# Spreading 128 expert dot products over two searches and a table, with gather buffers that hold no early chunks

## The reference, cut to what matters

```python
q = (xc @ w_query).reshape(C, PEER_HEADS, 2, PEER_HALF)
sc = jnp.einsum('thpd,hpnd->thpn', q, sub_keys)
top_s, top_i = lax.top_k(sc, PEER_TOPK)
cand_s = (top_s[:, :, 0, :, None] + top_s[:, :, 1, None, :]).reshape(C, PEER_HEADS, PEER_TOPK * PEER_TOPK)
cand_i = (top_i[:, :, 0, :, None] * PEER_NKEYS + top_i[:, :, 1, None, :]).reshape(...)
best_s, best_pos = lax.top_k(cand_s, PEER_TOPK)
experts = jnp.take_along_axis(cand_i, best_pos, axis=-1)
gates = jax.nn.softmax(best_s, axis=-1)
u, vv = expert_down[experts], expert_up[experts]
act = jax.nn.gelu(jnp.einsum('cd,chkd->chk', xc, u), approximate=False)
return jnp.einsum('chk,chkd->cd', gates * act, vv)
```

## Time and profile before

| | us |
|---|---|
| median of 3 runs | 1519.17 |
| lowest and highest | 1518.54, 1522.5 |
| profiled execution, its own time | 1524.2 |
| its span | 1522.4 |

### The profile page before, as it was taken

The page is one execution under the profiler, slowest core; times in us unless marked ns, Lnnn a source line. Parts: engine busy times, 40 slices in busy tenths (PEclk is TensorE's granted clock), DMA queues, the critical chain, the costliest instruction groups (busy, mean ns, idle before and its releaser), DMA issues. The chain is left out here.

```text
span 1522.4 us, 24797 instructions
## 1 busy us (share of the span) xinstructions
PE 1409.8 (93%) x8327; PEld 1212.7 (80%) x8327; DVE 993.1 (65%) x2325; ACT 636.8 (42%) x1256; POOL 205.5 (13%) x170
## 2 busy tenths in 40 slices
PE   7998989997896758999999999999999999989998
PEld 4665689997796658777777777789999999659994
DVE  4666569977996567566666666665555555256761
ACT  2433242017750005433333333356665665326651
POOL 0000164325876420000000000000000000000000
PEclk9999999999997988999999999999999999999999
DMA  8330187898999992365656556485554443236630
GB/s 299 133 137 1 46 333 263 314 386 307 404 409 409 409 403 85 99 191 181 191 188 185 192 182 191 138 249 176 178 153 153 152 152 111 91 89 193 183 90 28
DMA packets 145527, 307.17 MB, mean 202 GB/s; under 512 B 39968, under 2 KB 89632, under 8 KB 143904
## 3 DMA queue, kind: packets, MB, share of 16 engines
q1 hardware_dynamic: 127008, 238.93, 46.9%
q0 software_dynamic: 18432, 67.12, 11.5%
HBM read 304.73 MB, written 1.29 MB: 201 GB/s over the span
## 5 line engine op out<-in xcount | busy, mean ns | idle before, releaser
L1331 PE MATMUL plain_u<-whole,ring 128*128 128x128 f32 x1760 | 218.3, 285 | 34.6 <-DMA ring<-in_downT 34.6
L1331 PEld LDWEIGHTS plain_u<-whole,ring 128*128 128x128 f32 x1760 | 210.8, 200 | 40.2 <-DMA ring<-in_downT 40.0
L1882 ACT ACTIVATE hT_high<-ring 128x1024 fp32r<-128x1024 f32 x128 | 135.8, 1061 | 224.8 <-PE experts_acc L247 223.7
L245 PE MATMUL experts_acc<-hT_high,experts_wh 128*128 128x512 f32 x512 | 204.5, 399 | 1.5 <-DVE hT_low L1898 1.5
L246 PE MATMUL experts_acc<-hT_low,experts_wh 128*128 128x512 f32 x512 | 203.2, 397 | 0.0
L247 PE MATMUL experts_acc<-hT_high,experts_wl 128*128 128x512 f32 x512 | 203.2, 397 | 0.0
L1682 DVE CUSTOM_DVE_ANT_0 table<-table,h_row 128x1024 f32<-128x1024 f32 x128 | 152.3, 1223 | 45.1 <-DMA table<-in_down_rows,select_expert 41.6
L1459 POOL DMA_INDIRECT table<-in_down_rows,select_expert x128 | 161.6, 1262 | 145.1 <-DVE select_u L1682 101.4
L1898 DVE TENSOR_TENSOR hT_low<-ring,hT_high 128x1024 fp32r<-128x1024 f32 x128 | 156.9, 1226 | 27.4 <-ACT hT_high L1882 27.4
L245 PE MATMUL mix_a_pj<-mix_a_wh,hT_high 128*128 128x384 f32 x368 | 129.1, 351 | 0.0
L245 PEld LDWEIGHTS experts_acc<-hT_high,experts_wh 128*128 128x128 f32 x512 | 96.6, 189 | 35.2 <-issue 7.5
(11 more groups left out here) (393 smaller groups left out, 2601.9 us busy)
## 6 DMA issues: line engine op xcount, KB each, us to landing
ring<-in_up SPq DMA_DIRECT2D x128, 512.0 KB, 3.5
ring<-in_downT SPq DMA_DIRECT2D x110, 512.0 KB
mix_raw<-in_wa SPq DMA_DIRECT2D x46, 768.0 KB, 6.2
block_w_raw<-in_w SPq DMA_DIRECT2D x16, 768.0 KB, 6.2
mix_raw<-in_wb SPq DMA_DIRECT2D x16, 768.0 KB, 6.7
ring<-in_route SPq DMA_DIRECT2D x16, 576.0 KB, 5.2
table<-in_downT SPq DMA_DIRECT2D x18, 512.0 KB, 6.0
wo<-in_wo SPq DMA_DIRECT2D x4, 1024.0 KB, 7.9
```

What stands on the lines that cost most here:

```text
L245: pe.matmul(out, lhs[0], rhs[0], start=start, stop=False, skip_group_check=True)
L1331: mm = pe.matmul(self.u[g % 2][:, i * P:(i + 1) * P], rows[:, k, :], self.h[:, k, P:SEQ], start=k == 0, stop=k == KD - 1, skip_group_check ...
L1882: act.activation(uh[b % 2], raw_u[b], ACT.Copy).then_inc(u_high, 1)
```

## The change

It has four parts.

1. `FREE` = 12: none of the 12 gather buffers holds an early chunk. `EARLY` becomes 6 (was 18), the POOL waits for chunks in the first 12 gathers are gone, and SP issues none of the chunks ahead of the weights (`first` is 0 instead of 6), then one behind each of the first six weights. Chunks 6 and 7 go into the two free ring buffers behind the last weight.
2. `AHEAD` = 60 (was 56) chunks before the slot transposes, so 20 instead of 24 beside the first table.
3. The dot products are placed anew: the two choices come as before; 6 dot products stand in the first search itself, 29 in the second, 3 after the gates (38 in all up to the transposes, where there were 16), then 1 and 2 in turn in the 17 rounds of the table (25, where there were 51), and 65 in the last ten rounds (where there were 61). All use the same code; `dots` now takes a count.
4. `begun` follows (63), and with it the pacing of SP.

```diff
-EARLY = GATHERS + 6
+FREE = 12
+EARLY = GATHERS - FREE + 6
-AHEAD = 56
+AHEAD = 60
-DOTS_FIRST, DOTS_HALVES, DOTS_INDEX, DOTS_TURN, DOTS_GROUP = 4, 1, 3, 2, 3
+DOTS_FIRST, DOTS_LISTS, DOTS_PAIRS, DOTS_INDEX, DOTS_TURN = 2, 2, 3, 5, 3
+DOTS_SEARCH = 3 * DOTS_FIRST + 2 * DOTS_PAIRS + 4 * DOTS_LISTS + 3 * DOTS_INDEX + DOTS_TURN
...
-    begun = DOTS_FIRST + 4 * DOTS_HALVES + 2 * DOTS_INDEX + DOTS_TURN + DOTS_GROUP * (GROUPS + 1)
+    begun = DOTS_SEARCH + sum(1 + g % 2 for g in range(GROUPS + 1))
...
-            first = EARLY - (HP - NW)
+            first = max(0, EARLY - (HP - NW))
...
-                chunks.load(sp, first + hp - NW)
+                if first + hp - NW < EARLY:
+                    chunks.load(sp, first + hp - NW)
...
-                if s < GATHERS:
-                    pool.wait_ge(chunks.projected, EARLY_ROWS + s + 1)
-                else:
+                if FREE <= s < GATHERS:
+                    pool.wait_ge(chunks.projected, EARLY_ROWS + s - FREE + 1)
+                elif s >= GATHERS:
...
-            for n in range(2):
-                for h in range(4 * n, 4 * n + 4):
-                    halves(0, h)
-                    if n == 0:
-                        halves(1, h)
-                pairs(0, n)
-                indices(0, n)
-                choose(n)
-            at = DOTS_FIRST
-            dots(0, at)
-            for n in range(2):
-                for h in range(4 * n, 4 * n + 4):
-                    if n == 1:
-                        halves(1, h)
-                        dots(at, at + DOTS_HALVES)
-                        at += DOTS_HALVES
-                pairs(1, n)
-                indices(1, n)
-                dots(at, at + DOTS_INDEX)
-                at += DOTS_INDEX
+            for h in range(4):
+                halves(0, h)
+                halves(1, h)
+            pairs(0, 0)
+            indices(0, 0)
+            choose(0)
+            at = 0
+            for h in range(4, HEADS_P):
+                halves(0, h)
+                if h > 4:
+                    at = dots(at, DOTS_FIRST)
+            pairs(0, 1)
+            indices(0, 1)
+            choose(1)
+            at = dots(at, DOTS_INDEX)
+            pairs(1, 0)
+            at = dots(at, DOTS_PAIRS)
+            indices(1, 0)
+            at = dots(at, DOTS_INDEX)
+            for h in range(4, HEADS_P):
+                halves(1, h)
+                at = dots(at, DOTS_LISTS)
+            pairs(1, 1)
+            at = dots(at, DOTS_PAIRS)
+            indices(1, 1)
+            at = dots(at, DOTS_INDEX)
...
-                dots(at, at + DOTS_GROUP)
-                at += DOTS_GROUP
+                at = dots(at, 1 + g % 2)
...
-            left = SLOTS - at
+            left = SLOTS - begun
...
-                         for b in range((GATHERS, EARLY - GATHERS)[t])] for t in range(NT)]
+                         for b in (range(FREE, GATHERS), range(EARLY - GATHERS + FREE))[t]] for t in range(NT)]
```

More of the change, by code:

```diff
@@ L1675, in choose, with dots @@
                 dve.tensor_copy(expert[:, at], number[:, at]).then_inc(chosen, 1)
-            def dots(lo, hi):
-                for s in range(lo, hi):
+            def dots(lo, n):
+                for s in range(lo, lo + n):
                     b = s % GATHERS
@@ L1682, in dots @@
                     dve.tensor_tensor_reduce(gathered[b], gathered[b], h_row[:], 1.0, 0.0, ALU.mult, ALU.add, u[:, s:s + 1]).then_inc(dotted, 1)
+                return lo + n
             def digit(t, n, part):
@@ L1771, in _ @@
             last.then_inc(cols_ready, 1)
-            dots(at, at + DOTS_TURN)
-            at += DOTS_TURN
+            at = dots(at, DOTS_TURN)
             dve.wait_ge(cols_turned, 2)
@@ L1790, in _ @@
                 join(g, late_gelu[g - first])
-            left = SLOTS - at
+            left = SLOTS - begun
             for n, g in enumerate(range(middle, last)):
-                dots(at + left * n // (last - middle), at + left * (n + 1) // (last - middle))
+                at = dots(at, left * (n + 1) // (last - middle) - left * n // (last - middle))
                 join(g, late_gelu[(g - first) % WAITING])
```

## The result

The changed kernel takes 1535.86 us (median of 4 runs, 1532.82 to 1539.37); the kernel before, run beside it, takes 1520.15 (4 runs). The ratio is 1.0099, 95% interval 1.0077 to 1.0121: it is slower by 15 us, and outside the range (1509 to 1529). The profiled execution took 1532.82 us with a span of 1531.0. Its end lies only 8.6 us behind the one of before, while the last gather lies 13.9 us behind; the medians differ by 15.7, so the last gather is the better marker, and the profiled execution of before took some 5 us more than the changed one behind it.

What follows compares the result with a forecast made beforehand. Bound by empty DMA time before the last gather: 19.6 + 3 + 14 + 6.5 + 1 = 44.1 us against 44.8, so that gather lands 0.9 us earlier and the median is 1518.3 us, no change; range 1509 to 1529.

Steps and rivals of the forecast that it cites:

- What bounds the kernel: Up to the last gather: empty DMA time decides, 44.8 us before the change, with 342.5 us of transfers in both kernels.
- The queries: Queries and first search: they end 10 us earlier, first gather at 237.5, but 19.6 us of DMA empty instead of 13.7.
- I count 3 us empty ... From 248 us on both queues have work: After the first gather: 3 us of DMA empty (bounds 1.5 and 5), then gathers and chunks both queue from 248 us.
- TensorE ... reaches 60 at about 370: Before the slot transposes: TensorE finishes 60 chunks at 369.5 us against 347.4, so the first table starts 22 us later.
- The search's end: VectorE's search with 35 dot products takes 107 us, ending near 343, and near 352 with the gates and 3 more dots.
- The first table: The 15 table groups take 61 us, 63 up to the joins instead of 83.8; joins start at 445.3.
- The rival with 4.7 us a group: First table shrinks too little: 70.5 us instead of 61, kernel at 1527.8; chance 0.30, including 0.02 for the low clock.
- 14 us are empty: Beside the first table: 57.6 us of transfers wanted in 71.7 us, so 14 us of DMA time empty.
- 6.5 at the joins: At the joins, with buffers full and chunk 88 waiting for 69 dots: 6.5 us of DMA empty (bounds 0 and 9).
- The account of gains and losses: Up to the last gather: 44.1 us empty against 44.8, so it lands at 570.4 instead of 571.3, 0.9 us earlier.
- The later start eats the whole gain of the shorter table: First table: starts 22 us later, is 20.8 us shorter, so the joins start at 445.3 against 444.1.
- The rule of the low clock: TensorE waiting for DMA before its matmuls runs at the low clock, reaching its 60th chunk some 40 us later; chance 0.02.

Runs made afterwards that it cites:

- x_pace: The changed kernel, but each of the first 12 gathers (gather s) waits until chunk s has been multiplied: ratio 1.0066 to the kernel before.
- x_mid_four: The kernel before with 4 of 12 gather buffers free of early chunks and 26 (not 16) dot products before the slot transposes: ratio 0.9899.
- x_free: The kernel before with only the 12 gather buffers freed of early chunks; old dot products and 56 chunks: ratio 1.0014.
- x_four: The kernel before with 4 gather buffers freed of early chunks and nothing else: ratio 0.9968.
- x_burst: The kernel before, but the first twelve gathers all wait until 14 chunks are multiplied and then go back to back: ratio 1.0074.
- x_dots: The kernel before with only the new places of the dot products (38 before the slot transposes): ratio 1.0008.
- the pair: The changed kernel with 56 instead of 60 chunks before the slot transposes: ratio 1.0060; with the first 12 gathers also paced by chunks, 1.0043.

## Why the prediction was wrong, point by point

- **What bounds the kernel** was right: the empty DMA time before the last gather accounts for when that gather comes, within 1.7 us in 16 of 17 kernels. My count of it for the changed kernel was wrong: 44.1 us up to the last gather, where it is some 58 (56.1 to 550 us and 2.2 behind).
- **The queries** (19.6 us empty to 237, and the 3 that follow) were right: 21.8 to 240. The 19.6 is a slip, 34 from 53 leaves 19; two more, without effect, are the 373.6 (240 + 133.3 is 373.3) and the 5.4 us a group, where the rows have 5.2. The weights' wait went, and the first gather came within 1.3 us.
- **"I count 3 us empty ... From 248 us on both queues have work"** failed. 240 to 290 us holds 8.2 more empty us. From 244 to 264 us gathers alone pass: SyncE issues no chunk between 235.4 and 264.65 us, though by TensorE's rows chunk 6, whose buffer it waits for, is through at about 249.4 (in x_pace at 248.6, and there SyncE issues at 248.74). 3 of the 8.2 are the crawl: x_pace has 5.0. With 240 to 355 us filled I had 90 transfers; x_pace moved 23.65 + 21.15 MB, 85.4 transfers, the changed kernel 83.
- **"TensorE ... reaches 60 at about 370", of which I took 369.5, is the step that failed: 380.74.** Of the 11.2 us, 3.6 are the crawl (377.14 in x_pace). For the rest compare x_pace at 355 us: I had 8.5 chunks to go at 1.79 us each, that is, with the gather buffers already full. Ten were to go, and the buffers weren't full: six came at 2.50 us (354.89 to 369.90) and only the last four at 1.81. The 1.5 chunks make 2.7 us and the slower six 4.3; with 0.7 by which I rounded down, 11.3. My own count had 50 gathers moved by 355 us; 45 had been (23.65 MB).
- **The search's end** was late too (348.6 at L1762 instead of near 343), harmless, since VectorE then waited 19.70 us.
- **The first table** was right: 61.6 us from first to last eviction (61), so 4.11 us apart, joins 2.35 us later. The rival with 4.7 us a group, to which I gave the slower side, did not happen; the kernel is slower by another way.
- **"14 us are empty" in the table, and 6.5 at the joins**, together with 1 of small losses 21.5, were 28.5 between 372 us and the last gather. The split was off in both places. From 372 to the first join at 457.6 us 25.4 us are empty: 1.6 up to the transposes, 8.9 up to the first eviction and 15.0 beside the table. Behind it there are 3 instead of 7.5. The 11.4 us too many in the table's stretch match the 11.2 by which it starts late: the gather buffers were full before the transposes (the last gather ahead of them is issued at 363.21, and from 373.5 chunks come at full speed), and in the 24 us until a dot product frees one, only the few chunks that TensorE takes can be moved.
- **The account of gains and losses.** "The later start eats the whole gain of the shorter table" took the 22 us as exact; at 33 the balance is gone. The last gather landed 14.7 us later than my 570.4; the joins account for 12.3 of it (457.6 instead of 445.3). As a ledger: 21.8 + 8.2 + 25.4 + 3 = 58.4 empty, against my 44.1.
- **The rule of the low clock**, to which I gave 0.02, did not apply: 290 to 350 us, where TensorE waits half a microsecond for nearly each chunk, shows a granted clock of 1.00. The section that the prediction names in the Trainium skill (TensorE: Matmul & The Clock Gate, "Loop structure matters more than you think") shows a long wait ahead of every matmul going with the low clock, and the prediction left the "long" out; these waits are short.

The general fault: I treated three parts as adding up in one ledger and weighed none of them alone. Once all buffers are full, every transfer that the parts have brought ahead of the table is missing beside it, and each puts off the table's start, while its own demand (20 chunks and 25 gathers, 57.6 us of transfers) can't fill the 85.6 us from 372 up to the joins.

## What to carry to other kernels

Where transfers bound a stretch, count its empty microseconds by window and spread demand so that no window runs dry; what fills a hole early is missing from a later window once all buffers are full. When a queue runs ahead, ask at what rate the other side is served *until* the buffers are full, not after. Of a resource that can be freed in steps, try the small step: 4 buffers of 12 gave more than 12. And weigh the parts of a change alone and in pairs before trusting their sum.

## What the runs showed of the hardware that was not expected

Several engines can stand still for "issue" behind a run of gathers, with their data there. In the changed kernel, from 244 to 264 us, gathers alone are moved, and a single instruction packet passes; in x_pace three pass beside them (queues, packets, MB, share of the engines' time; the changed kernel, then x_pace):

```profile
q0 software_dynamic: 1983, 7.23, 98.1%
q14 instruction: 1, 0.01, 0.1%
```

```profile
q0 software_dynamic: 1299, 4.74, 65.0%
q1 hardware_dynamic: 659, 2.43, 31.7%
q8 instruction: 1, 0.02, 0.3%
q14 instruction: 2, 0.02, 0.2%
```

x_mid_four, without a crawl, has the gathers at 92.3% in the same 20 us, and three instruction packets:

```profile
q0 software_dynamic: 1812, 6.62, 92.3%
q8 instruction: 2, 0.03, 0.6%
q14 instruction: 1, 0.01, 0.1%
```

So it is not the presence of gathers but, it seems, their backlog: GpSimd issues one per 1.24 us at best (1.35 on average for the 18 up to 261.67 us), and at 363 GB/s (245 to 264 us) one takes 1.44 us, just the time from one burst of matmuls to the next. How long it lasts goes with how many gathers are issued in one run. With 12 unpaced and 38 dots, which free buffers for 6 gathers more, it is 18 us; with 12 and the old dots (x_free) about 10; with 8 it is 5.3; with 4 (x_mid_four, x_four) it is absent, and x_burst brings it into the old kernel. x_dots, with no free buffer, has a trace of it too (5 pauses, 2.0 us, from 275 to 279). Pacing the gathers gives back 0.33% in the changed kernel, 0.32% in x_free and 0.17% in the pair, uncertain by 0.2 to 0.3 each; pacing also lets chunks pass among the first gathers, and no run parts this from the crawl. TensorE's granted clock falls with the crawl, to 0.66 in 245 to 264 us (x_pace: 1.00), which belongs to the price.

That late instruction packets are the cause is argued, not shown: no run changed the instructions alone. For it speaks that the one packet passes between 263 and 264 us, when the crawl ends, and four engines go on within 1.1 us of each other: TensorE at 263.74, VectorE at 264.54, SyncE at 264.65 and ScalarE, with the GELU of chunks 4 to 7, at 264.82. Against it: 30 matmul rows run in the 17 us before with no such packet, and a low count alone does no harm, since in x_pace none passes from 300 to 320 us and TensorE has no wait for issue there.

The Trainium skill (Runtime: NRT & Kernel Launch, section "Instruction fetch mechanics") says that each sequencer fetches its next instructions through a DMA queue of its own while it runs the current ones, and that the cost is mostly hidden. In the kernel before the trace agrees (no wait for issue in TensorE's chunks from 235 to 290 us); behind a backlog of gathers there are 8.2 us of such waits in 12 pauses, which disagree with it if they are waits for instructions, and that isn't shown.

The even share of two full queues held wherever both were full, a chunk each 2.56 us beside a gather each, 1.28 us a transfer. The Trainium skill (DMA: Bandwidth & Descriptors, section "Queues, rings and completion order") has each engine take turns between its queues packet by packet; with packets of like size (3.64 and 3.65 KB on average in x_pace, 240 to 355 us) that is this share, and the trace agrees with the share; the turns themselves it doesn't show.
